# Two transformer blocks at float32 on one core: post-norms from PSUM by pieces, out and down projections tile by tile, branches bank by bank, constant products ahead of long waits

## What is computed

```python
# first block, cut to what the change touches
x = x + mx[2] * (jnp.concatenate([att_x, hg_x], -1) @ w_out[l])
x = x + mx[5] * swiglu(modulate(rmsnorm(x, g_norm2[l]), mx[3], mx[4]), w_gu[l], w_down[l])
x = rmsnorm(x, g_final)
# second block
o_a = moba_attention(...) @ w_branch_a[l]
o_b = mla_attention(...) @ w_branch_b[l]
merged = gates[..., :D_MODEL] * o_a + gates[..., D_MODEL:] * o_b
x = x + _rms_norm(merged @ w_out[l], g_post_mix[l])
h2 = _rms_norm(x, g_pre_mlp[l])
m = jnp.square(jax.nn.relu(h2 @ w_up[l])) @ w_down[l]
x = x + _rms_norm(m, g_post_mlp[l])
```

## Time and profile before

| | us |
|---|---|
| median of 3 runs (lowest, highest) | 972.46 (971.69, 974.57) |
| the profiled execution's own time | 974.37 |
| its span on the core | 971.4 |
| PE busy | 881.0 (91%) |
| PE weight load busy | 740.6 (76%) |
| DVE, ACT, POOL busy | 424.2 (44%), 419.3 (43%), 413.1 (43%) |
| mean granted TensorE clock, of full speed | 0.941 |
| share of the span in the chain that ended last: PE, DVE, issue, ACT | 75%, 12%, 5%, 4% |
| DMA, mean | 150 GB/s |

### The profile page before, as it was taken

One profiled execution on the slowest core, in us unless ns is written; L12 is line 12 of the kernel. 1 busy time (PEld: TensorE's weight loads), 2 busy tenths in 40 slices (PEclk: granted clock), 3 DMA queues, 4 the chain that ended last, 5 costly groups with the idle time before them and its releaser, 6 DMA issues.

```text
span 971.4 us, 14105 instructions
## 1 busy us (share of the span) xinstructions
PE 881.0 (91%) x5427; PEld 740.6 (76%) x5427; DVE 424.2 (44%) x641; ACT 419.3 (43%) x648; POOL 413.1 (43%) x199
## 2 busy tenths in 40 slices
PE   4999896979999699999997799999998599999995
PEld 3678775865547589999996688778796489999994
DVE  3554464893250633232334425453317643344334
ACT  4344212124534434344444464554474444544442
POOL 2434000000015246657463688443384455665652
PEclk9999987989959899999999699999999789999998
DMA  9773744115613245566653377333254236565541
GB/s 311 239 247 90 251 149 142 45 44 174 173 36 116 87 136 182 184 192 185 198 177 100 131 203 184 110 93 102 88 153 135 81 119 203 176 192 176 193 151 44
DMA packets 93531, 145.52 MB, mean 150 GB/s; under 512 B 15403, under 2 KB 63760, under 8 KB 93488
## 3 DMA queue, kind: packets, MB, share of 16 engines
q1 hardware_dynamic: 92608, 143.23, 47.4%
q0 software_dynamic: 848, 1.70, 0.6%
q10 hardware_dynamic: 32, 0.01, 0.0%
HBM read 143.87 MB, written 1.05 MB: 149 GB/s over the span
## 4 chain that ended last, share of the span: by engine, by line
PE 75%; DVE 12%; issue 5%; ACT 4%; POOL 2%; DMA 2%; SPq 0%; DVEq 0%; ACTq 0%; POOLq 0%
PE bank L1525 73%; ACT w_hi L647 1%; DMA raw<-in_w_mod 1%; PE bank L1779 1%; POOL w_lo L592 1%; DVE h_f L1123 1%; POOL z_lo L621 1%; PE bank L2068 1%; DMA raw<-in_w_in 1%; DVE yn L1489 1%; DVE merged_lo L1476 1%; DVE x L1495 0%; DVE hg_kb L1216 0%; DVE hg_kf L1216 0%; DVE hg_at L1227 0%
## 5 line engine op out<-in xcount | busy, mean ns | idle before, releaser
L592 POOL TENSOR_TENSOR w_lo<-raw,w_hi 128x1024 fp32r<-128x1024 f32 (+2 forms) x163 | 392.6, 2422 | 521.0 <-ACT w_hi L647 499.8
L647 ACT ACTIVATE w_hi<-raw 128x1024 fp32r<-128x1024 f32 (+1 forms) x218 | 226.9, 1044 | 238.9 <-PE bank L1525 199.4
L1061 DVE TENSOR_TENSOR w_lo<-raw,w_hi 128x1024 fp32r<-128x1024 f32 x58 | 74.5, 1294 | 138.1 <-ACT w_hi L647 137.9
L1525 PE MATMUL bank<-z_hi,w_hi 128*128 128x256 f32 x384 | 111.8, 291 | 2.4 <-POOL z_lo L621 2.4
L1525 PE MATMUL bank<-z_lo,w_hi 128*128 128x256 f32 x384 | 110.3, 287 | 0.0
L1525 PE MATMUL bank<-z_hi,w_lo 128*128 128x256 f32 x384 | 110.2, 287 | 0.0
L1525 PE MATMUL bank<-n_hi,w_hi 128*128 128x256 f32 x352 | 100.2, 285 | 1.4 <-DVE w_lo L1061 0.5
L1525 PE MATMUL bank<-n_lo,w_hi 128*128 128x256 f32 x352 | 98.9, 281 | 0.0
L1525 PE MATMUL bank<-n_hi,w_lo 128*128 128x256 f32 x352 | 98.8, 281 | 0.0
L1525 PE MATMUL bank<-w_hi,mlp_h_hi 128*128 128x512 f32 x216 | 84.9, 393 | 2.9 <-DVE mlp_h_lo L1511 1.5
L1525 PE MATMUL bank<-w_lo,mlp_h_hi 128*128 128x512 f32 x216 | 84.7, 392 | 0.0
(11 more groups left out here) (361 smaller groups left out, 1674.8 us busy)
## 6 DMA issues: line engine op xcount, KB each, us to landing
raw<-in_w_in SPq DMA_DIRECT2D x54, 512.0 KB, 4.6
raw<-in_w_down SPq DMA_DIRECT2D x54, 512.0 KB, 3.7
raw<-in_w_gu SPq DMA_DIRECT2D x44, 512.0 KB, 3.5
raw<-in_w_mod SPq DMA_DIRECT2D x32, 512.0 KB, 4.2
raw<-in_w_up SPq DMA_DIRECT2D x32, 512.0 KB, 3.7
raw<-in_w_mod SPq DMA_DIRECT2D x32, 256.0 KB, 6.2
raw<-in_w_out SPq DMA_DIRECT2D x12, 512.0 KB, 3.5
raw<-in_w_in SPq DMA_DIRECT2D x8, 336.0 KB, 2.9
```

Source lines behind the costliest of these rows:

```text
L592: nc.gpsimd.tensor_tensor(wl[:, w % SPL, 0:size], raw[:, slot_raw, 0:size], wh[:, w % SPL, 0:size].bitcast(F32), ALU.subtract).then_inc(s_ ...
L647: nc.scalar.activation(wh[:, w % SPL, 0:size], raw[:, slot_raw, 0:size], ACT.Copy).then_inc(s_hi, 1)
L1061: V.tensor_tensor(wl[:, w % SPL, :], raw[:, slot_raw, :], wh[:, w % SPL, :].bitcast(F32), ALU.subtract).then_inc(s_lod, 1)
L1525: return nc.tensor.matmul(out_, l, r_, start=start, stop=stop, skip_group_check=True)
```

## The change

It has these parts. (1) keep_clock issues n float32 products of the identity by 256 constant columns into a bank that is free, ahead of a wait: 13 after the first block's out, 9, 1, 4 and 5 in the "z" norm, 6 between branches and out, 1, 4, 4 and 5 in the "y" norm. (2) The last two chunks of a branch go together, so that its banks end one after the other, each with a signal; DVE multiplies bank by bank. The low parts of A3 and B3 move from POOL to DVE. (3) ACT takes A3 after two gates instead of four; before the merge it has only B3 and O0, then O1 and O2 ahead of its rounding of piece 2, and O3 ahead of that of piece 4. (4) In the last step of each out and down projection the loop over the halves j lies outside that over the chunks, so that its four banks end one after the other. (5) The post-norm squares a bank when it is done; the sum's first half goes in as the logarithm's bias; DVE multiplies the bank by the gain ahead of the reciprocal root, and one instruction per half scales and adds. The last output leaves in four DMAs.

```diff
@@ by_dve
-                    or c2 in (-2, -1) or ...
+                    or w in (W2["branch a"] - 1, W2["branch b"] - 1) or c2 in (-2, -1) or ...
@@ SP
             for t in range(2):
-                sp.wait_ge(DV.sem, DV[f"x5 {t}"])
-                sp.dma_start(out[0, P * t:P * t + P, :], x[:, t, :]).then_inc(s_out, 16)
+                for j, made in enumerate((f"x5 {t} first", f"x5 {t}")):
+                    sp.wait_ge(DV.sem, DV[made])
+                    sp.dma_start(out[0, P * t:P * t + P, 512 * j:512 * j + 512], x[:, t, 512 * j:512 * j + 512]).then_inc(s_out, 16)
@@ ACT
                 nc.scalar.activation(gates[:, j, :], gates[:, j, :], ACT.Sigmoid, bias=bgc[:, j:j + 1]).then_inc(AC.sem, AC.tick(f"gate {j}"))
-                if j % 4 == 3:
+                if j == 1:
+                    hi2(45)
+                elif j % 4 == 3:
                     hi2(45 + j // 4)
-            hi2(52)
+            hi2(50)
             for b, (k0, k1) in enumerate(MERGED):
-                if b >= 3:
-                    hi2(50 + b)
+                if b in (2, 4):
+                    hi2(51 + b // 2)
                 act.wait_ge(DV.sem, DV[f"merged {b}"])
...
-                    waits[t]()
                     for j in range(2):
+                        if t and j:
+                            all_made()
+                        else:
+                            made(t, j)
...
-                    act.wait_ge(DV.sem, DV[f"ss {name} {t}"])
-                    ln_exp(act, 68 + t, 210 + t, 1, D, f"{name} {t}")
+                    act.wait_ge(AC.sem, AC[f"sq{name} {t} 1"])
+                    act.wait_ge(DV.sem, DV[f"half {name} {t}"])
+                    nc.scalar.activation(stat[:, 68 + t:69 + t], stat[:, 65 + 2 * t:66 + 2 * t], ACT.Ln, bias=stat[:, 210 + t:211 + t],
+                                         scale=1.0 / D).then_inc(AC.sem, AC.tick(f"ln {name} {t}"))
@@ DVE
+            branch_lo("branch a")
             for b in range(4):
                 dve.wait_ge(AC.sem, AC[f"gate {2 * b + 1}"])
-                if b == 0:
+                if b == 3:
                     dve.wait_ge(s_used, W2["branch a"])
+                else:
+                    dve.wait_ge(PE.sem, PE[f"branch 0 {2 * b + 1}"])
                 tick(V.tensor_tensor(flat(mgf, 2 * b, 2), ps[b][:], flat(gates, 2 * b, 2), ALU.mult), f"ma {b}")
+            branch_lo("branch b")
             for b, (k0, k1) in enumerate(MERGED):
...
-                if b == 0:
+                if k1 == KT:
                     dve.wait_ge(s_used, W2["branch b"])
+                else:
+                    dve.wait_ge(PE.sem, PE[f"branch 1 {(k1 - 1) | 1}"])
...
+                def gained(t, j):
+                    dve.wait_ge(AC.sem, AC[f"sq{name} {t} {j}"])
+                    tick(V.tensor_tensor(yn[:, t, 512 * j:512 * j + 512], ps[bank + 2 * t + j][:],
+                                         gpost[:, gain, 512 * j:512 * j + 512], ALU.mult), f"{name} g {t} {j}")
...
+                def added(t):
                     for j in range(2):
+                        c = slice(512 * j, 512 * j + 512)
+                        own(f"{name} g {t} {j}")
+                        tick(V.scalar_tensor_tensor(out=x[:, t, c], in0=yn[:, t, c], scalar=stat[:, 216 + t:217 + t], in1=x[:, t, c],
+                                                    op0=ALU.mult, op1=ALU.add), outs[t] if j else f"{outs[t]} first")
+                half(0)
+                gained(0, 0)
+                mean(0)
+                gained(0, 1)
+                refined(0)
+                added(0)
+                half(1)
+                gained(1, 0)
+                mean(1)
+                gained(1, 1)
+                refined(1)
+                added(1)
@@ PE
+            def keep_clock(bank, n):
+                for _ in range(n):
+                    mm(ps[bank][:, 0:T], ident, cst[:, 0:T], True)
@@ rows_out (hidden_out alike: for its last step t, j, q)
                         for t in range(2):
-                            for kk in ks:
-                                for j in range(2):
+                            for j in range(2):
+                                for kk in ks:
...
             pe.wait_ge(AC.sem, AC["ga2 1"])
+            keep_clock(4, 13)
...
-            def rows_by_channel(name, made):
+            def rows_by_channel(name, made, bursts):
                 for t in range(2):
+                    keep_clock(*bursts[t])
                     pe.wait_ge(DV.sem, DV[f"{made} {t}"])
...
+                keep_clock(*bursts[2])
                 pe.wait_ge(DV.sem, DV[f"{name} diag 1"])
                 mm(ps[0][:, 0:T], ones, dg[:].rearrange("p t k -> p (t k)"), True).then_inc(PE.sem, PE.tick(f"{name} rstd"))
+                keep_clock(*bursts[3])
-            rows_by_channel("z", "x3")
+            rows_by_channel("z", "x3", ((3, 9), (3, 1), (3, 4), (3, 5)))
...
-                for k in range(4):
-                    s = next2()
+                for ks in ((0,), (1,), (2, 3)):
+                    slots = {k: next2() for k in ks}
                     for j in range(8):
-                        ins = mm3(...)
-                    ins.then_inc(s_used, 1)
+                        for k, s in slots.items():
+                            ins = mm3(...)
+                            if j == 7:
+                                ins.then_inc(s_used, 1)
+                            elif k == 3:
+                                ins.then_inc(PE.sem, PE.tick(f"branch {m} {j}"))
             pe.wait_ge(DV.sem, DV["ma 3"])
+            keep_clock(0, 6)
...
-            rows_by_channel("y", "x4")
+            rows_by_channel("y", "x4", ((4, 1), (1, 4), (1, 4), (1, 5)))
```

More of the change, by code:

```diff
@@ L483, in by_dve @@
             return (12 <= w < W_END["g"] or c1 in (2, 3) or (4 <= c1 < 4 + 12 * MLP1_TRIPS and (c1 - 4) % 6 >= 4)
-                    or c2 in (-2, -1) or (2 <= c2 < 2 + 12 * MLP2_TRIPS and (c2 - 2) % 12 in (2, 3, 8, 9)))
+                    or w in (W2["branch a"] - 1, W2["branch b"] - 1) or c2 in (-2, -1) or (2 <= c2 < 2 + 12 * MLP2_TRIPS and (c2 - 2) % 12 in (2, 3, 8, 9)))
         def low_made(eng, w, i=0):
@@ L978, in _, with post_norm @@
             load_functions(LN_EXP)
-            def post_norm(name, waits, banks):
+            def post_norm(name, made, all_made, banks):
                 for t in range(2):
-                    waits[t]()
                     for j in range(2):
+                        if t and j:
+                            all_made()
+                        else:
+                            made(t, j)
                         if t or j:
@@ L997, in _ @@
             hi_mlp2(0)
-            post_norm("7", (lambda: act.wait_ge(PE.sem, PE["out 2 0"]), lambda: act.wait_ge(s_used, W2["out"])), range(4))
+            post_norm("7", lambda t, j: act.wait_ge(PE.sem, PE[f"out 2 {t} {j}"]), lambda: act.wait_ge(s_used, W2["out"]), range(4))
             for t in range(2):
@@ L1028, in _ @@
             h2_hi(3 * MLP2_TRIPS)
-            post_norm("9", (lambda: act.wait_ge(PE.sem, PE["mlp 2 0"]), lambda: act.wait_ge(s_used, M0W + 4 + 12 * MLP2_TRIPS)), range(4, 8))
+            post_norm("9", lambda t, j: act.wait_ge(PE.sem, PE[f"mlp 2 {t} {j}"]),
+                      lambda: act.wait_ge(s_used, M0W + 4 + 12 * MLP2_TRIPS), range(4, 8))
         @block.vector
@@ L1313, in _ @@
             dve.wait_ge(AC.sem, AC["ga2 1"])
-            dve.wait_ge(PE.sem, PE["out 0"])
+            dve.wait_ge(PE.sem, PE["out 0 1"])
             for t in range(2):
@@ new lines, in half, with mean @@
+                def half(t):
+                    dve.wait_ge(AC.sem, AC[f"sq{name} {t} 0"])
+                    tick(V.tensor_scalar(stat[:, 210 + t:211 + t], stat[:, 64 + 2 * t:65 + 2 * t], 1.0 / D, EPS, ALU.mult, ALU.add),
+                         f"half {name} {t}")
+                def mean(t):
+                    s_, h_, v = (stat[:, c:c + 1] for c in (65 + 2 * t, 210 + t, 212 + t))
+                    dve.wait_ge(AC.sem, AC[f"sq{name} {t} 1"])
+                    own(f"half {name} {t}")
+                    tick(V.scalar_tensor_tensor(out=v, in0=s_, scalar=1.0 / D, in1=h_, op0=ALU.mult, op1=ALU.add), f"{name} v {t}")
@@ new lines, in refined @@
+                def refined(t):
+                    r_, v, e = (stat[:, c:c + 1] for c in (68 + t, 212 + t, 214 + t))
+                    dve.wait_ge(AC.sem, AC[f"rstd {name} {t}"])
+                    own(f"{name} v {t}")
+                    done(V.scalar_tensor_tensor(out=e, in0=r_, scalar=v, in1=r_, op0=ALU.mult, op1=ALU.mult), f"{name} e {t}")
+                    done(V.tensor_scalar(e, e, -0.5, 1.5, ALU.mult, ALU.add), f"{name} f {t}")
+                    done(V.tensor_tensor(stat[:, 216 + t:217 + t], r_, e, ALU.mult), f"{name} r {t}")
@@ L1879, in rows_out @@
                                               kk == 0, kk == KT - 1)
-                                if t:
-                                    ins.then_inc(s_used, 1)
```

(16 more changed lines are left out.)

29 lines of the change are left out of this document (11 added, 18 removed).

## The result

**Measured.** 966.91 us median (965.89 to 967.96, 5 runs) against 973.38 for the kernel before in the same session (971.69 to 974.57, 5 runs): ratio 0.9934, 95% interval 0.9919 to 0.9949. That is 6.5 us faster, a small gain but clear of the noise. The forecast was 967.1, from a gain of 5.4 and the earlier median of 972.46. The profiled execution has a span of 964.1 us against 971.4, 7.3 less.

A forecast was written before the change was run, and what follows sets the result against it. PE bounds the kernel, standing still in four gaps with a low clock after them. Terms 0.4 + 0.5 - 1.8 + 3.7 + 2.6 = 5.4 us took 972.5 to 967.1; range 963.5 to 971.8.

The forecast's parts named there:

- Norm after the first out: Norm after the first block's out: transposes at full clock let DVE start 0.4 us sooner; gain 0.4, ends 0 and 0.8.
- "z" norm: Norm producing z: product of ones by the diagonals and its hand-over take half as long; gain 0.5 us, ends 0 and 1.
- POOL is not faster, so the clock itself gives nothing: Behind the z norm: PE's third weight group needs POOL, so full clock on the first two groups gains nothing.
- Branches, merge, out: Branches, merge and out: branches end 1.5 us later, ACT's order delays O3 and O4; loss 1.8, ends gain 3.6, loss 4.
- sum of piece 2 held by POOL on O1: In out: DVE's sum of merged piece 2 waits for POOL's low part of O1 until 734.8.
- The theory is wrong if out's stage gets shorter: Sign for out: from the end of branch b to out's last matmul, 28.5 us instead of 28.2.
- ACT's order now costs: In out: O3's high part now stands behind ACT's rounding of piece 3; PE waits 1.5 for O3, 1.7 for O4.
- "y" norm: Norm after out, and up behind it: diagonal 1.8 sooner, ones product 0.4, up's half clock 1.5; gain 3.7, ends 1.5 and 6.
- End: Last post-norm and store: x of tile 1 2.2 us sooner, smaller last DMA 0.4; gain 2.6, ends 2.0 and 3.7.
- rival 1: After out, POOL on U1 precedes DVE's second half; the y norm gives about 0.5 instead of 3.7: 970.3; chance 25%.
- Rival 2: Out as meant: O3 and O4 aren't late, port order falling the other way; stage gains 1.8: 963.5; chance 10%.
- Rival 3: The constant products don't hold PE's clock, decided in the z norm; slower by 4.9, 977.4; chance 6%.

The follow-up runs named there:

- products alone: The kernel before with only the constant products (keep_clock and its calls) added: 971.77 us, ratio 0.9978 to the kernel before.
- the new order alone: The changed kernel with every constant product (keep_clock call) removed: 970.37 us, ratio 0.9968 to the kernel before.
- pieces alone: The changed kernel without constant products and with the old order of branches and rounding, leaving the new post-norms: 968.64 us, ratio 0.9949 to the kernel before.
- the kernel with the short products: The changed kernel with the zero products ahead of both MLP loops in bf16, one pass instead of four: 966.20 us, ratio 0.9919 to the kernel before.

## Why the prediction was right, point by point

The time was right within 0.2 us and most of the mechanisms too. That it was so close is partly luck. The gain was 6.5 us and not 5.4, and the kernel before came out at 973.38 this time instead of the 972.46 that I started from. Within the sum, a loss of 1.55 us that I didn't see is made up by gains that were priced too low and a loss (out) that was priced too high.

- **Norm after the first out:** 0.4 forecast, 0.46 measured. The 13 products fit.
- **"z" norm:** 0.5 forecast, 0.50 measured. The step that failed is the sentence "POOL is not faster, so the clock itself gives nothing": it gives less than nothing. PE at full clock reaches the third group 2.5 us early, the clock fell within 0.7 us of the end of that wait in six of seven executions, and 1.3 to 1.6 us were lost (0 where it didn't fall). A faster engine in front of the same bound turned time at work into idle time, and I priced only the time won.
- **Branches, merge, out:** a loss of 1.8 forecast, 0.96 measured. In the branches the forecast holds: 1.5 later (1.53), waits of 0.46 for POOL (0.6 forecast) and of 0.59 for DVE ahead of the pair (0.8 forecast). O4's wait was 1.6 (1.7 forecast), O3's 0.5 (1.5 forecast), because POOL was done with O3 at 741.2; my chain had 743.1, less the 0.9 by which this trace is ahead there. The step that failed is "sum of piece 2 held by POOL on O1": the sum ran free in 0.69 us at 730.84, 0.15 us ahead of POOL. What I also had wrong is how the branches and out join: the branches' delay is no term of its own. With it taken away out ends 0.1 sooner. By my own sign ("The theory is wrong if out's stage gets shorter") this part fails: from the last of branch b to the last of out I forecast 28.5 instead of 28.2 us, and it went from 28.1 to 27.5. What costs is ACT's order, which I named ("ACT's order now costs"), and more than the stage shows: undoing it gives 2.3. The parts of the loss don't add up: the six products alone cost 0.7 (51.76), the new order alone 0.9 (52.03), both together 0.96.
- **"y" norm:** 3.7 forecast, 4.3 measured (2.84 and 1.45). The halves landed 0.2 and 0.4 us ahead of my times, and the second diagonal at +8.3 instead of +8.95 (766.01 - 757.74). The runs split it: pieces alone give 2.36 in the norm and lose 1.0 in up (8.36), products alone give 0.5 and 1.5. That is 1.4 and 2.0 alone and 4.3 together: the earlier norm pays in full only where up finds the full clock.
- **End:** 2.6 forecast, 3.09 measured: x at +4.0 instead of +4.5, and from there to the end 2.5 us instead of 3.1, so what I put at 0.4 for a store of half the size was 0.6.
- **Zero products:** "I take nothing from it" stands for most executions; single ones differ by 1.1 at either place.
- **Rivals:** rival 1 didn't happen, by a margin of 0.02 us. Rival 2 happened by half: of its two places the order on the ports fell the other way at the first (the sum of piece 2 above) and not at the second (the last piece's sum was held, 2.53 us), and the stage still lost. With O3 and O4 no longer behind ACT's rounding the kernel took 964.4, where that rival said 963.5. Rival 3 is refuted: the clock read 1.00 from 758 to 768, and in both norms.
- **The two sides of the sum.** Forecast 5.4 on the profiled execution. The change's own part, by stretches, is 0.46 + 0.50 - 1.55 - 0.96 + 4.29 + 3.09 = 5.8; 1.15 lost and 2.6 won by chance make up the 7.3.

## What to carry to other kernels

Filling waits to hold the clock paid where the engine behind the wait isn't bounded by another one (up behind the "y" norm), and not where it is (behind the "z" norm, out); behind the filled stretch, look for the next wait that the faster clock opens, and fill or remove that too. An order on one in-order engine (here ACT: rounding ahead of the next chunk's high part) can close a ring through two others; move the instruction that starts the other engine ahead of the one that waits for it. Split a span into stretches before comparing two traces: here chance moved the span by more than most parts of the change.

## What the runs showed of the hardware that was not expected

- Code that was the same in all kernels took 321.2 to 326.0 us, and the clock fell in other places from one execution to the next (half clock until 290.5 in the trace before, until 283.1 in the one after). That this is the whole difference isn't shown.
- The same idle 2.5 us of PE was followed by half clock in six executions and by full clock in one.
- Ahead of both MLP loops PE's clock fell in all twelve executions: while the products of one row ran (3.7 to 5.0 us) or up to 1.5 us behind them, and in the kernel with the short products (1.0 us, then PE idle for 3.1) 3.4 and 1.1 us behind them.
- Half the clock in the old order of out cost nothing measurable (23.86 with 3.4 us of it, twice, and 24.56 without, twice): POOL's and ACT's chain set the pace.
